# Second front of a two-block transformer kernel: split products for 44 weight units, gv with tokens moving, and a reordered norm

## The reference

```python
n = rmsnorm_2(h, norm_mix)
c_q, c_kv, k_pe, gq, gk, gv, ga, gg, gate_a, gate_b = split(n @ w_in)
q  = rmsnorm_2(c_q, q_norm) @ w_uq          # 8 heads of 128 + 64
kv = rmsnorm_2(c_kv, kv_norm) @ w_ukv       # 8 heads of 128 + 128
y_a = block_causal_attention(norm(q_nope), rope(q_pe), norm(k_nope), rope(k_pe), v)
y_b = rmsnorm_2(gated_linear_attention(gq, gk, gv, log_sigmoid(ga @ w_a2 + b_a) / 16), g_norm) * silu(gg)
mix = sigmoid(gate_a) * (y_a @ w_o_mla) + sigmoid(gate_b) * (y_b @ w_o_gla)
h = h + mix @ w_out
h = h + peer_ffn(rmsnorm_2(h, norm_ffn))
```

## Time and profile before

| | |
|---|---|
| runs, us | 2389.84, 2378.21, 2385.87 (median 2385.87) |
| profiled execution, us | 2377.14, span 2375.3 |
| busy share of the span | TensorE 97%, VectorE 68%, ScalarE 51%, GpSimd 18% |
| TensorE's mean granted clock | 0.99 of 2.4 GHz |

### The profile page before, as it was taken

How to read it: one execution, slowest core, us unless ns; L and a number is a source line. 1 busy time by engine, 2 the same in 40 slices (tenths; PEclk the granted TensorE clock), 3 DMA queues, 4 the chain that set the end, 5 groups by cost and what they waited for, 6 DMA issues and landing times.

```text
span 2375.3 us, 46821 instructions
## 1 busy us (share of the span) xinstructions
PE 2311.1 (97%) x14976; PEld 2072.6 (87%) x14976; DVE 1625.0 (68%) x3596; ACT 1214.2 (51%) x2620; POOL 432.6 (18%) x263
## 2 busy tenths in 40 slices
PE   8999899999999999999999999999999999999999
PEld 3788799999998888888777678889999999888887
DVE  4764458888788777776135774257888879777776
ACT  4555255555586555554125322045555577555554
POOL 0000000766671000000000000000467772000000
PEclk9999999999999999999999899999999999999999
DMA  8676345777654666665434223454677764666665
GB/s 323 237 248 214 132 160 179 184 181 184 185 125 153 212 211 216 210 215 165 142 125 141 72 82 103 162 177 160 182 182 185 179 150 134 208 209 209 209 209 167
DMA packets 191110, 422.77 MB, mean 178 GB/s; under 512 B 54288, under 2 KB 88336, under 8 KB 190624
## 3 DMA queue, kind: packets, MB, share of 16 engines
q1 hardware_dynamic: 150112, 413.73, 52.9%
q0 software_dynamic: 36864, 0.15, 4.3%
q10 hardware_dynamic: 4032, 7.64, 0.9%
HBM read 403.48 MB, written 17.96 MB: 177 GB/s over the span
## 4 chain that ended last, share of the span: by engine, by line
PE 92%; DVE 4%; ACT 2%; issue 1%; DMA 1%; DVEq 0%; ACTq 0%
PE ps L1558 20%; PE ps L779 19%; PE ps L1552 12%; PE ps L1553 12%; PE ps L1554 12%; PE ps L1559 10%; PE ps L1848 2%; PE ps L1222 1%; PE ps L859 1%; PE ps L1244 1%; PE ps L1590 1%; DMA ring<-stream 1%; PE ps L1236 0%; DVE gbuf L871 0%; PE ps L1480 0%
## 5 line engine op out<-in xcount | busy, mean ns | idle before, releaser
L1558 PE MATMUL ps<-csplit,hl 128*128 128x512 f32 x2048 | 718.7, 396 | 7.1 <-issue 6.1
L1772 POOL DMA_INDIRECT gates<-gbuf,picks_at x256 | 431.2, 1684 | 1512.5 <-issue 1061.4
L1552 PE MATMUL ps<-hsplit,hl 128*128 128x256 f32 x2304 | 658.1, 286 | 9.6 <-DVE hsplit L968 4.6
L1553 PE MATMUL ps<-hsplit,hl 128*128 128x256 f32 x2304 | 653.5, 284 | 0.0
L1554 PE MATMUL ps<-hsplit,hl 128*128 128x256 f32 x2304 | 653.5, 284 | 0.0
L1559 PE MATMUL ps<-csplit,hl 128*128 128x256 f32 x2048 | 575.0, 281 | 0.0
L1629 ACT CAST hl<-ring 128x512 fp32r<-128x512 f32 x562 | 344.2, 620 | 311.2 <-PE ps L1554 274.5
L1632 DVE TENSOR_TENSOR hl<-ring,hl 128x512 fp32r<-128x512 f32 x562 | 386.6, 693 | 142.7 <-ACT hl L1629 107.8
L1558 PEld LDWEIGHTS ps<-csplit,hl 128*128 128x128 f32 x2048 | 384.6, 188 | 98.3 <-issue 7.2
L1552 PEld LDWEIGHTS ps<-hsplit,hl 128*128 128x128 f32 x2304 | 443.5, 192 | 11.2 <-issue 10.7
L1553 PEld LDWEIGHTS ps<-hsplit,hl 128*128 128x128 f32 x2304 | 444.1, 193 | 0.0
(11 more groups left out here) (238 smaller groups left out, 1992.2 us busy)
## 6 DMA issues: line engine op xcount, KB each, us to landing
ring<-stream SPq DMA_DIRECT2D x675, 512.0 KB
s_area<-stream SPq DMA_DIRECT2D x48, 512.0 KB, 5.1
gates<-zeros SPq DMA_DIRECT2D x32, 512.0 KB, 5.1
gring<-gates SPq DMA_DIRECT2D x256, 64.0 KB, 4.1
gates<-gbuf,picks_at POOLq DMA_INDIRECT x256
arena<-xc ACTq DMA_DIRECT2D x2, 1024.0 KB, 15.6
arena<-keys ACTq DMA_DIRECT2D x2, 1024.0 KB, 4.7
gbuf<-consts ACTq DMA_DIRECT2D x1, 1120.0 KB, 5.6
```

Of the source, the lines that this page charges most:

```text
L1552: pe.matmul(out_ap, w[0], m[0], start=start, stop=False)
L1553: pe.matmul(out_ap, w[1], m[0], start=False, stop=False)
L1558: pe.matmul(ps[:, bank, :], w_hi, m_both, start=start, stop=False)
L1772: pool.indirect_dma_start(out=cells, out_offset=bass.IndirectOffsetOnAxis(ap=picks_at[:, i, c:c + 1], axis=0), in_=gates[:, i, c:c + 1], i ...
```

## The change

Three things change.

First, 20 input units (ckv, kpe, gq, gk, ga, uq, ukv_k) and all 24 output units (wo_mla, wo_gla, w_out) are multiplied as three passes of split weights and inputs, as the PEER loops do. `split_weights` makes the high half of a unit on ScalarE (into one of three places, `whi`) and the low half on VectorE, over the unit's own place in the ring. It is queued two units ahead of the products (`SPLIT_LEAD`), at the point where `take_tiles` comes to the tile of that unit; wo_mla's first two units are split in the attention and behind it. The inputs n2, cqn, ckvn, the attention's outputs, the GLA output and the mixed value are split too, each by a ScalarE copy and a VectorE subtraction.

Second, gv is multiplied with tokens moving: eight fp32 tiles of 272 columns, whose results are turned by TensorE (three transposes each) and copied by ScalarE in two halves (`act_gv_keep`). The decay now waits for the second half (`gv_kept`).

Third, the order: the rest of the `once` norm moves into the middle of uq, the multiplication by silu is cut into four, wo_mla's splits are placed around GLA's copies, and two products of zeros come at the start of TensorE's queue.

```diff
+    ring_lo, _ = place("ring_lo", [P, RING, UNIT], F32R, at=ring_at)
...
+    n2_hi, n2_lo = parted("n2_hi", "knope_n", KD, TM), parted("n2_lo", "v2", KD, TM)
...
+    WHI = 3
...
+    SPLIT_LEAD = 2
...
+    def split_tile(group, unit, ready, hi, lo, cols, engine, take, k=KD, at=0, words=UNIT):
+        if unit not in split_units:
+            split_units.append(unit)
+            split_words.append(words)
+            split_first.append(len(tiles))
+            j = len(split_units) - 1
+            if unit not in (units["ckv"][0], units["ckv"][1], units["wo_mla"][0], units["wo_mla"][1]):
+                split_at.setdefault(split_first[j - SPLIT_LEAD], []).append(j)
+        j = split_units.index(unit)
+        low = ring_lo[:, place_of[unit], :]
+        pairs = []
+        for i in range(k):
+            c = slice(at + i * P, at + (i + 1) * P)
+            pairs.append((whi(j)[:, c], low[:, c], hi[:, i, :], lo[:, i, :]))
+        tile(group, unit, ready, pairs, P, cols, engine, take)
+        tiles[-1].split = j
+    def split_weights(kind, eng, j):
+        u, n = split_units[j], split_words[j]
+        if kind == "act":
+            eng.wait_ge(S(arrival(u)[0]), arrival(u)[1])
+            same = [i for i in range(j) if whi(i).offset == whi(j).offset and whi(i).tensor.name == whi(j).tensor.name]
+            if same:
+                eng.wait_ge(S("tile_done"), last_tile[split_units[same[-1]]] + 1)
+            eng.copy(whi(j)[:, 0:n], slot(u)[:, 0:n]).then_inc(S("w_hi"), 1)
+        else:
+            eng.wait_ge(S("w_hi"), j + 1)
+            eng.tensor_tensor(ring_lo[:, place_of[u], 0:n], slot(u)[:, 0:n], whi(j)[:, 0:n].bitcast(F32), ALU.subtract)\
+               .then_inc(S("w_lo"), 1)
...
+    group3("ckv", ckv_b, ("n2_split", 1), n2_parts, TM)
+    split_tile("kpe", units["kpe"][0], None, *n2_parts, TM, "act", take_copy(kpe_raw))
...
+    group3("gq", gq, None, n2T_parts, T, make=gq_take)
+    group3("gk", gk, None, n2_parts, TM)
+    split_tile("ga", units["ga"][0], None, *n2_parts, TM, "act", take_copy(ga_b))
...
-            tile("uq", u, ("cq_ready", 1), std_pairs(u, cqn, 3, at=s * 3 * P), P, T, "act", take_copy(dst))
+            split_tile("uq", u, ("cqn_split", 1), cqn_hi, cqn_lo, T, "act", take_copy(dst), k=3, at=s * 3 * P, words=6 * P)
...
-    group2("ukv_k", knope, ("ckv_ready", 1), ckvn, TM, k=2, per=4)
+    group3("ukv_k", knope, ("ckvn_split", 1), (ckvn_hi, ckvn_lo), TM, k=2, per=4)
...
+    def gv_take(i):
+        def f(kind, eng, src):
+            wait(eng, "gv_turned", i - 1)
+            return eng.copy(gv_rows[:, i % 2, :], src)
+        return f
+    gv_tile, gv_seq = [], []
     for i, u in enumerate(units["gv"]):
-        for t, (a, n) in enumerate(KT2):
-            tile("gv", u, None, v_pairs(u, n2, a, n), n, P, "act", take_copy(gv[0:n, t, i * P:(i + 1) * P]))
-    gv_taken = taken["act"]
+        tile("gv", u, None, std_pairs(u, n2), P, TM, "act", gv_take(i))
+        gv_tile.append(len(tiles) - 1)
+        gv_seq.append(taken["act"])
...
+        split_tile("wo_mla", u, None, attn2_hi, attn2_lo, T, "dve", wo_mla_take(n))
+    tiles[group_of["wo_mla"][0]].each = ("attn2_split",)
     for n, u in enumerate(units["wo_gla"]):
-        tile("wo_gla", u, ("gla_ready", 1), std_pairs(u, og_n), P, T, "dve",
-             add_take(mixed2[:, n, :], sgate_b[:, n, :], rs2[:, n % 2, 0:T]))
-    mixed2_taken = taken["dve"]
+        split_tile("wo_gla", u, None, og_hi, og_lo, T, "dve",
+                   add_take(mixed2[:, n, :], sgate_b[:, n, :], rs2[:, n % 2, 0:T]))
+    tiles[group_of["wo_gla"][0]].each = ("og_split",)
     for n, u in enumerate(units["w_out"]):
-        tile("w_out", u, ("taken_dve", mixed2_taken), std_pairs(u, mixed2), P, T, "dve", resid_take(n, None))
+        split_tile("w_out", u, None, mixed2_hi, mixed2_lo, T, "dve", resid_take(n, None))
+    tiles[group_of["w_out"][0]].each = ("mixed2_split",)
+    mixed2_first = tiles[group_of["wo_gla"][0]].seq
...
+            if t.split is not None:
+                pe.wait_ge(S("w_lo"), t.split + 1)
...
+                if t.split is not None:
+                    w_hi, w_lo, x_hi, x_lo = pair
+                    mm = passes(pe, ps[0:t.rows, t.bank, 0:t.cols], (w_hi, w_lo), (x_hi, x_lo), i == 0, i == last)
+                    continue
...
+            for j in split_at.get(n, ()):
+                split_weights(kind, eng, j)
...
+    GV_GROUPS = ((0,), (1,), (), (2,), (3,), (), (4,), (5,), (), (6,), (7,), ())
+    GV_HALF = 4
+    def pe_gv_turn(pe, i):
+        pe.wait_ge(S("taken_act"), gv_seq[i])
+        if i == GV_HALF:
+            pe.wait_ge(S("gv_kept"), 1)
+        for t, (a, n) in enumerate(KT2):
+            mm = pe.transpose(ps[0:n, 4 + t, i % GV_HALF * P:(i % GV_HALF + 1) * P], gv_rows[:, i % 2, a:a + n], ident)
+        mm.then_inc(S("gv_turned"), 1)
+    def act_gv_keep(act, half):
+        act.wait_ge(S("gv_turned"), GV_HALF * (half + 1))
+        for t, (a, n) in enumerate(KT2):
+            ins = act.copy(gv[0:n, t, half * 512:(half + 1) * 512], ps[0:n, 4 + t, :])
+        ins.then_inc(S("gv_kept"), 1)
+    def gv_fill(kind, eng, g):
+        for i in GV_GROUPS[g]:
+            if kind == "pe":
+                pe_tiles(eng, gv_tile[i:i + 1])
+                if i:
+                    pe_gv_turn(eng, i - 1)
+            else:
+                take_tiles("act", eng, gv_tile[i:i + 1])
+                if i == GV_HALF:
+                    act_gv_keep(eng, 0)
+        if g == len(GV_GROUPS) - 1:
+            if kind == "pe":
+                pe_gv_turn(eng, len(gv_tile) - 1)
+            else:
+                act_gv_keep(eng, 1)
...
-            for n, r in enumerate((self.both, self.once)):
-                act.wait_ge(S("norm_inverted"), self.g0 + n + 1)
-                act.sqrt(r, r).then_inc(S("norm_rooted"), 1)
+            act.wait_ge(S("norm_inverted"), self.g0 + 1)
+            act.sqrt(self.both, self.both).then_inc(S("norm_rooted"), 1)
+            for k in range(KD):
+                act.wait_ge(S("n2_ready"), k + 1)
+                act.copy(n2_hi[:, k, 0:T], n2[:, k, 0:T]).then_inc(S("n2_hi"), 1)
+            act.wait_ge(S("n2_meta"), 1)
+            act.copy(n2_hi[:, :, T:TM], n2[:, :, T:TM]).then_inc(S("n2_hi"), 1)
+        def act_once(self, act):
+            act.wait_ge(S("once_inverted"), 1)
+            act.sqrt(self.once, self.once).then_inc(S("once_rooted"), 1)
+        def dve_once(self, dve):
+            dve.reciprocal(self.once, self.once).then_inc(S("once_inverted"), 1)
+            dve.wait_ge(S("once_rooted"), 1)
+            for k in range(KD):
+                ins = dve.scalar_tensor_tensor(resid[:, k, :], resid[:, k, :], v_("final", k), self.once, ALU.mult, ALU.mult)
+            chain(ins, dve)
...
-            chain(dve.tensor_scalar(once, once_sums[:, 0:T], 1.0 / D, EPS, ALU.mult, ALU.add), dve)
-            dve.reciprocal(once, once).then_inc(S("norm_inverted"), 1)
-            dve.wait_ge(S("norm_rooted"), self.g0 + 2)
+            dve.tensor_scalar(once, once_sums[:, 0:T], 1.0 / D, EPS, ALU.mult, ALU.add).then_inc(S("norm_inverted"), 1)
             for k in range(KD):
-                ins = dve.scalar_tensor_tensor(resid[:, k, :], resid[:, k, :], v_("final", k), once, ALU.mult, ALU.mult)
-            chain(ins, dve)
+                dve.wait_ge(S("n2_hi"), k + 1)
+                dve.tensor_tensor(n2_lo[:, k, 0:T], n2[:, k, 0:T], n2_hi[:, k, 0:T].bitcast(F32), ALU.subtract)
+            dve.wait_ge(S("n2_hi"), KD + 1)
+            dve.tensor_tensor(n2_lo[:, :, T:TM], n2[:, :, T:TM], n2_hi[:, :, T:TM].bitcast(F32), ALU.subtract)\
+               .then_inc(S("n2_split"), 1)
...
+        def dve_part(self, eng, x):
+            raw, hi, lo = self.parts
+            eng.wait_ge(S("attn2_hi"), x + 1)
+            eng.tensor_tensor(lo[:, x, :], raw[:, x, :], hi[:, x, :].bitcast(F32), ALU.subtract).then_inc(S("attn2_split"), 1)
...
+                    if self.parts:
+                        x = it["copy"]
+                        eng.wait_ge(S("attn_out_ready"), self.o0 + x + 1)
+                        eng.copy(self.parts[1][:, x, :], dst).then_inc(S("attn2_hi"), 1)
...
+        dve_gla_level(dve, i)
+        if i == 14:
+            split_weights("dve", dve, first_out)
+    def act_att2_step(act, i):
+        act_gla_level(act, i + 1)
+        if i == 12:
+            split_weights("act", act, first_out)
...
+        pe.wait_ge(S("gv_kept"), 2)
...
+        act.wait_ge(S("gla_kept"), len(gla_steps))
+        split_weights("act", act, first_out + 1)
+        take_tiles("act", act, group_of["wo_mla"][0:1])
         act.wait_ge(S("gla_turned"), 1)
         act.copy(kdecT[0][0:META, :, :], ps[0:META, 3, :].rearrange("p (h d) -> p h d", h=GLA_HEADS))
         act.copy(kdecT[1], ps[:, 6, :].rearrange("p (h d) -> p h d", h=GLA_HEADS)).then_inc(S("gla_turned_copied"), 1)
+        take_tiles("act", act, group_of["wo_mla"][1:4])
...
+    def act_part(act, ready, raw, hi, done):
```

(66 more changed lines are left out.)

111 lines of the change are left out of this document (77 added, 34 removed).

## The result

The changed kernel takes 2365.36 us in the median of 14 runs (2356.76 to 2377.07), the kernel before 2377.95 in 14 runs beside them: ratio 0.9947, 95% interval 0.9929 to 0.9965. That is 12.6 us or 0.53%, and the interval (0.35 to 0.71%) lies wholly on the faster side; by how much is known to some 4 us either way. The forecast was 2369: 16.3 us off the profiled execution of 2377.1, and 8.7 us added for the median of the three runs shown. The profiled spans are 2362.6 and 2375.3.

The account below looks back on a forecast made before the run. TensorE was taken as the bound, on 92% of the chain that ended last. Terms 6.8 + 8.2 - 4.5 + 6.4 + 1.6 - 2.2 = 16.3 us off 2377.1 gave 2360.8, plus 8.7 for a median 2369; range 2352 to 2384.

Parts of the forecast that it names:

- sum of 16.3 us: Whole change: gains and losses of all stages and clock effects together take 16.3 us off the profiled 2377.1.
- Price of a product: TensorE: a 256-column output tile falls from 3.48 to 2.88 us when split, saving 0.60; a 272-column one saves 0.64.
- Inputs: Input products: 11.5 us off TensorE, 4.7 paid back for splits and waits in uq, net gain 6.8 us.
- Arrival: Input units: transfer, splitting and tile allow 2.6 us per unit, above a uq unit's 2.16; cost 0 to 2, taken as 0.
- gv: gv stage: eight 272-column tiles instead of 24 small ones, 43.5 us against 51.7, gain 8.2; bounds 5 and 12.
- Clock around the decay: The gap moves from before norm_kn to before the decay, so norm_kn's first tile escapes the lower clock: gain 1.6 us.
- the gg tiles pay while another chain sets the end: Behind the decay: gg tiles take the lower clock's cost without setting the stage's end; part of the 1.6 us gain.
- Attention: Attention stage: ScalarE's output copies and the first output weight's split lose 4.5 us; bounds 0 and 7.
- Output products: Output stage: 14.4 us off TensorE, ending 6.4 us earlier, less 2.2 for wo_gla's slow first tile.
- the sum of 6.4: Output stage ends 6.4 us earlier before the slow-tile cost, with wo_gla at 3.4 us a tile and w_out gaining 4.2.
- Cold tiles: Slower rival: wo_gla and w_out's sixteen tiles stay at the lower clock, up to 2.88 us each, 46 us, 2415; chance 0.10.
- 34 us: Rival that all of it hides: input, gv and output savings of 11.5 + 8.2 + 14.4, giving 2352; chance 0.10.

Follow-up runs that it names:

- e8: Changed kernel with e3 and e4, og's low-half pieces ahead of the second wo_gla unit's low half, and gg tiles moved around the decay: 2347.65 us, ratio 0.9891.
- e12: e9 with products of zeros on TensorE, two ahead of norm_qn, two ahead of norm_kn, three ahead of wo_gla: 2343.23 us, ratio 0.9846.
- e4: Changed kernel with the second norm of x moved from the middle of uq to behind the ukv_k tiles: 2357.72 us, ratio 0.9925.
- e3: Changed kernel with ScalarE in wo_gla making the mixed value's high half of tile n-1 instead of tile n: 2358.31 us, ratio 0.9925.
- e6: e3 with five products of zeros between the last wo_mla tile and wo_gla: 2359.31 us, ratio 0.9928.
- e7: Changed kernel without the two products of zeros at its start: 2364.52 us, ratio 0.9951.
- e1: Changed kernel with its twenty input units whole (fp32) again and the second norm of x back under cq: 2367.15 us, ratio 0.9960.
- e5: Changed kernel with gv as before, 24 small products filling the twelve norm groups: 2374.77 us, ratio 0.9990.
- e11: Changed kernel with both input and output units whole, leaving gv's new form, buffer places and the zeros at the start: 2361.69 us, ratio 0.9928.
- e2: Changed kernel with all 24 output units whole again and silu's multiplication as one operation: 2362.81 us, ratio 0.9928.
- e9: e8 with the multiplication by silu on VectorE moved ahead of the last norm: 2344.89 us, ratio 0.9847.
- e10: e8 with six products of zeros in TensorE's stop before wo_gla: 2354.75 us, ratio 0.9886.

## Why the forecast was right, and where it was off

The forecast named the path, the price of a product and the stops in uq and ahead of wo_gla, and its sum of 16.3 us was 3.2 too high against the table. That 2369 lies only 3.6 us from 2365.36 is in part luck, twice over. The 8.7 us added for a median came from three runs; over 14 runs the kernel before is 2377.95, 0.8 above its profiled execution, so with a sound base the forecast would have been 2361.7, below the result and not above it. And in the sum, the attention came out 3.15 us cheaper than forecast, which covers half of the 6.3 us that the other stages missed.

How far a stage repeats, over all profiles that have it in the old or in the changed form (number of profiles in brackets; e8 to e12 only where their orders leave the stage alone):

| stage | old form, us | changed form, us |
|---|---|---|
| input products | 96.2 (3) | 90.9 to 93.3 (6) |
| gv | 51.7 and 53.3 (2) | 42.8 to 44.4 (11) |
| decay to norm_kn | 20.1 (2) | 21.8 to 22.0 (8) |
| norm_kn to the attention | 41.1 and 41.4 (2) | 38.5 in seven, 40.05 in the table's |
| attention to the GLA output | 118.7 to 120.1 (3) | 121.3 to 122.8 (11) |
| GLA output to norm_ffn | 101.1 (3) | 98.6 to 98.7 (5) |

- **Price of a product.** Eight times three passes take 2.83 to 2.84 us at 256 columns (2.88 from the earlier trace rows) and 3.03 at 272; whole tiles 3.45. Right.
- **Inputs, 6.8 forecast, 5.35 measured.** The handing over from cq to ckv is without a stop. The waits behind the second norm of x were forecast at 1.2 and 2.0 us and are 0.85 and 2.09; what was left out is the lower clock in the unit behind them, 1.55 us. e4 takes the whole back, 4.53. Arrival, taken as 0, is not quite 0: in the other profiles of this order the stage is up to 2.4 us longer, with ScalarE waiting longer for units in e3, e6 and e7. That the bus is full where a unit lands in 5.1 us is shown by no row; the DMA engines' share in the earlier trace rows is 0.22 to 0.49.
- **gv, 8.2 forecast.** 7.28 in the pair of profiles, in which the first tile took 5.36 us instead of 3.67; 8.97 where it didn't (42.75 in e1). Right, though the terms as written add up to 43.8, not 43.5, so that the forecast was 7.9. With e5 and e11 it is the part that carries the change.
- **Clock around the decay, +1.6 forecast, -0.65 measured in the pair, +0.7 to +0.9 in the seven other profiles of the same order.** The step that failed is "the gg tiles pay while another chain sets the end": the decay stage is 1.7 to 1.9 us longer in all eight. Before, gg's end had 4.0 us to norm_kn, of which ScalarE needs 2.4 behind the last tile (take and squares), so the cover was 1.6 us. After, the gg tiles end 19.41 us behind the decay's first product instead of 16.12. 3.29 less 1.6 is the 1.7 lost. The other half of the step held: norm_kn's first tile, slow before, is fast in seven of the eight profiles, which gives 2.6 us back, and the table's is the one in which it is slow and only 1.03 comes back. The timeline of the changed kernel, TensorE and ScalarE:

```profile
1249.24 2.93 PE L1557 MATMUL ps<-gbuf 16*128 16x272 f32 x8 [3.96 <-issue]
...
1268.69 0.38 ACT L572 ACTIVATE gbuf<-ps 128x256 f32<-128x256 f32 x1 [0.76 <-PE ps L883]
1268.97 2.01 ACT L987 ACTIVATE arena<-arena 128x2176 f32<-128x2176 f32 x1
...
1271.03 1.27 PE L1006 MATMUL ps<-arena,onesbuf 128*128 128x272 f32 x2 [2.38 <-ACT arena L987]
```

  The 5 us from norm_kn's first product (the third column from the end is the granted clock), in the changed kernel and in e2:

```profile
1271.00:1276.00 5.00, 4.97 (x16) 4.09 (x17) 2.29 (x2) 2.46 (x3) 0.00 (x0) 0.68 0.40 138
```

```profile
1269.20:1274.20 5.00, 4.94 (x23) 4.32 (x24) 2.56 (x3) 2.98 (x4) 0.00 (x0) 1.00 0.45 156
```

- **Attention, -4.5 forecast, -1.35 measured in the pair, -1.2 to -4.0 over all profiles.** The loss per item is right: from reciprocal to reciprocal 7.68 us with the copy of the high half where it was 7.24:

```profile
1394.15 0.16 DVE L1444 RECIPROCAL small<-small 128x1 f32<-128x1 f32 x1 [1.20 <-ACT gbuf L1471]
...
1401.83 0.16 DVE L1444 RECIPROCAL small<-small 128x1 f32<-128x1 f32 x1 [1.57 <-ACT gbuf L1471]
```

  Five items pay 0.44, and the first output weight's split costs 0.95 and 1.14: 4.3 us. But the way into the first item is 0.56 us shorter, two other gaps between items 0.68 and 0.40, and the way from the last item to the GLA output 1.47 (11.14 to 9.67); one gap is 0.21 longer. Together that is 2.9 us. Part of the last is the first wo_mla tile, which lies there. The two gaps are not the split's: in e11, with the output units whole, they are as short or shorter.
- **Output products, 4.2 forecast with the slow tile, 2.5 measured.** wo_gla begins 19.26 instead of 15.38 us behind norm_gla, 3.88 later, of which 2.32 are the tiles that came earlier: 1.56 net, where 1.1 was forecast. The first wo_gla tile is slow as forecast, 1.85 us for 2.2. Apart from it wo_gla gained 5.0 us, where the sum of 6.4 leaves 3.3 for it. Mis-sized is w_out, 0.85 instead of 4.2: the loop of 3.44 us was seen, but it was charged to wo_gla and taken to end there. Two units of lead moved its wait to the first w_out tile, with a slow clock behind it. e3 shows both terms.
- **Cold tiles, the slower rival.** Did not come: of the sixteen tiles one at the start of wo_gla and two of w_out ran slow. The waits of 0.36 us at the last wo_gla tiles left the clock at 1.00, and only the stop of 2.14 us let it fall, to 0.62 over the next 4.3 us. The Trainium skill (TensorE: Matmul & The Clock Gate, "HAM oscillation — how this bites in real kernels") describes a loop in which each wait for operands is longer than the work of a tile, and every tile starts at the lower clock. Waits of 0.36 us beside tiles of 2.84 are another case, so that page does not speak for the 2415.

Why so little came of 34 us: of the 14.4 us of the output units 1.3 are left in the pair and nothing over all profiles (e2), because attention, the chain from norm_gla to wo_gla and the first w_out tiles gave them back. With the orders of e8 the same stretch is 214.5 us long instead of 219.8 to 221.2 with whole units, so the split itself is worth 5.3 to 6.7 in that profile; the queues' order hid it.

What stays open: why the gaps in the attention shrank, and why the untouched stretches differ by up to 15 us from profile to profile.

## What to carry to other kernels

Where two engines prepare the operands of a third, follow their loop over as many rounds as the third has lead: a loop that is too slow costs nothing at first and then stops it at a later stage, with a clock penalty on top. Put work that isn't urgent (here the second norm of x) where the engine that does it has nothing queued behind it, and multiplications that can be done early into the waits before the chain. When spans differ by more than the effect, compare stages from first product to first product, undo one part at a time, and read each stage in every profile that has it, since one pair can show the wrong sign.

## What the runs showed of the hardware

The same stop gives a slow tile in some profiles and not in others. Ahead of norm_qn TensorE stands 2.48 us in every profile but e12's. The changed kernel's profile and e4's:

```profile
1204.81 0.70 PE L1006 MATMUL ps<-arena,onesbuf 128*128 128x256 f32 x2 [2.48 <-ACT arena L987]
1205.34 5.52 PE L883 MATMUL ps<-arena,ring 128*128 128x272 f32 x16
```

```profile
1196.79 0.70 PE L1006 MATMUL ps<-arena,onesbuf 128*128 128x256 f32 x2 [2.48 <-ACT arena L987]
1197.32 3.83 PE L883 MATMUL ps<-arena,ring 128*128 128x272 f32 x16
```

The granted clock of the 7.2 us from there is 0.76 in the first and 1.00 in the second. Of eleven profiles with the new gv form and nothing in that stop, five have a gv stage of 42.75 us and six one of 44.3 to 44.4. Stops of 2.4 to 2.7 us ahead of norm_kn go both ways as well: over the next 5 us the clock is 0.67 and 0.68 in e8 and in the changed kernel, and 1.00 in seven others; where the stop is 3.86 or 4.00 us it is down in all four (before, e5, e9, e10). So a gap of some 2.5 us has to be priced as a chance of 1.5 to 1.7 us, not as a fixed cost. Shorter stops are no safe ground either. 0.85 us in uq and 0.36 in wo_gla left the clock up; 1.76 us ahead of norm_ckv did so in ten of eleven profiles and not in e5 (0.66 over the next 5 us); and the stops of 1.54 and 0.94 us between norm_gla's products, the same to 0.01 us in all fourteen profiles, were followed by slow wo_mla tiles in three (0.59 from 1464.8 to 1468.0 in the changed kernel, where it cost nothing, since VectorE's chain sets the start of wo_gla). And a stop of 0.51 us with the eight small decay products behind it was followed by a gg tile of 5.41 us in e8 and one of 3.72 in e12, so the length of the last stop alone does not decide it.
